# Two transformer blocks on one core: unnormalised x transposed between products, norm roots in the PSUM copies, alternating accumulators in the down projection

## What is computed

```python
for l in range(2):                                     # first block
    h = rms_norm(x, norm1_g[l])
    q, k, v, gu, gv = split(h @ w_in[l])               # 3584 columns
    ...                                                # attention, gelu(gu), gelu(gv), gating
    x = x + mixed @ w_o[l]
    h = rms_norm(x, norm2_g[l])
    g, u = split(causal_conv3(h @ w_up[l]))            # 2 x 5632 columns, 44 feature tiles each
    x = x + (silu(g) * u) @ w_down[l]
# second block: mod = silu(c) @ w_ada + b_ada (12288 columns), the same for c_ctx
hc = rmsnorm(ctx, norm1_w) * (1 + csc1) + csh1         # context stream, 256 tokens
s_f, s_b = ssd_branch(hc, ...)                         # states only
hl = rmsnorm(x, norm1_w) * (1 + sc1) + sh1             # x stream
x = x + g1 * token_mixer(hl, s_f, s_b)
x = x + g2 * sqrelu_mlp(rmsnorm(x, norm2_w) * (1 + sc2) + sh2)
out = rmsnorm(x, final_norm_w)
```

## Time and profile before

| | |
|---|---|
| median of 3 runs | 3853.71 us (3839.27 to 3853.76) |
| the profiled execution | 3845.48 us, its span 3843.7 us |
| TensorE (PE) busy | 3568.9 us, 93% of the span |
| VectorE (DVE) busy | 2363.7 us, 61% |
| ScalarE (ACT) busy | 1608.2 us, 42% |
| DMA | 687.60 MB, mean 179 GB/s |
| mean granted TensorE clock | 0.961 of full speed |

### The profile page before, as it was taken

How to read it: one execution, slowest core, us unless ns; L and a number is a source line. 1 busy time by engine, 2 the same in 40 slices (tenths; PEclk the granted TensorE clock), 3 DMA queues, 4 the chain that set the end, 5 groups by cost and what they waited for, 6 DMA issues and landing times.

```text
span 3843.7 us, 43309 instructions
## 1 busy us (share of the span) xinstructions
PE 3568.9 (93%) x16122; PEld 2908.9 (76%) x16122; DVE 2363.7 (61%) x2921; ACT 1608.2 (42%) x2106; POOL 26.4 (1%) x26
## 2 busy tenths in 40 slices
PE   6978999998898979999998898999988889999998
PEld 5766888887776867888886777787853678888887
DVE  4766788886555765677776556237665555555554
ACT  4443454554333453555554333224421344344443
POOL 0000000000000000000000000000000000000000
PEclk9989999999999989999999999979999999999999
DMA  6635577775666636577775664336600445656564
GB/s 209 185 110 201 181 226 225 231 229 180 192 224 210 194 114 219 181 229 233 232 229 184 193 235 148 85 104 198 186 1 0 159 144 189 188 190 187 191 189 149
DMA packets 357795, 687.60 MB, mean 179 GB/s; under 512 B 24591, under 2 KB 28704, under 8 KB 356384
## 3 DMA queue, kind: packets, MB, share of 16 engines
q1 hardware_dynamic: 357664, 685.82, 55.9%
HBM read 683.64 MB, written 2.10 MB: 178 GB/s over the span
## 4 chain that ended last, share of the span: by engine, by line
PE 61%; issue 20%; DVE 8%; DMA 5%; ACT 3%; DVEq 1%; SPq 1%; POOL 0%; ACTq 0%; POOLq 0%
PE acc L1836 14%; PE acc L1838 14%; PE acc L1837 14%; PE acc L2066 4%; PE acc L2067 4%; PE acc L2068 4%; DMA w_raw<-in_w_down 3%; DVE w_lo L1075 2%; DMA w_raw<-in_w_in 1%; DVE ada_sum L1150 1%; ACT w_hi L687 1%; PE turn L2006 1%; PE acc L2303 1%; DMA w_raw<-in_w_o 1%; PE side L2313 1%
## 5 line engine op out<-in xcount | busy, mean ns | idle before, releaser
L1075 DVE TENSOR_TENSOR w_lo<-w_raw,w_hi 128x1024 fp32r<-128x1024 f32 x708 | 843.1, 1222 | 500.9 <-ACT w_hi L687 462.3
L687 ACT ACTIVATE w_hi<-w_raw 128x1024 fp32r<-128x1024 f32 x708 | 744.1, 1061 | 970.3 <-DMA w_raw<-in_w_up 358.3
L1836 PE MATMUL acc<-w_hi,in_h 128*128 128x512 f32 x2112 | 840.6, 398 | 25.3 <-DVE w_lo L1075 14.0
L1838 PE MATMUL acc<-w_hi,in_l 128*128 128x512 f32 x2112 | 830.1, 393 | 0.0
L1837 PE MATMUL acc<-w_lo,in_h 128*128 128x512 f32 x2112 | 829.8, 393 | 0.0
L1836 PEld LDWEIGHTS acc<-w_hi,in_h 128*128 128x128 f32 x2112 | 401.9, 190 | 113.7 <-issue 21.0
L1838 PEld LDWEIGHTS acc<-w_hi,in_l 128*128 128x128 f32 x2112 | 401.0, 190 | 85.7
L1837 PEld LDWEIGHTS acc<-w_lo,in_h 128*128 128x128 f32 x2112 | 401.9, 190 | 81.5
L2066 PE MATMUL acc<-w_hi,in_h 128*128 128x512 f32 (+1 forms) x1024 | 408.1, 399 | 19.9 <-issue 8.2
L2067 PE MATMUL acc<-w_lo,in_h 128*128 128x512 f32 (+1 forms) x1024 | 402.7, 393 | 0.0
L2068 PE MATMUL acc<-w_hi,in_l 128*128 128x512 f32 (+1 forms) x1024 | 402.6, 393 | 0.0
(11 more groups left out here) (299 smaller groups left out, 3719.9 us busy)
## 6 DMA issues: line engine op xcount, KB each, us to landing
w_raw<-in_w_up SPq DMA_DIRECT2D x352, 512.0 KB, 3.8
w_raw<-in_w_mlp SPq DMA_DIRECT2D x256, 512.0 KB, 3.6
w_raw<-in_w_in SPq DMA_DIRECT2D x200, 512.0 KB, 3.8
w_raw<-in_w_ada SPq DMA_DIRECT2D x192, 512.0 KB, 4.6
w_raw<-in_w_down SPq DMA_DIRECT2D x176, 512.0 KB, 5.0
w_raw<-in_w_o SPq DMA_DIRECT2D x64, 512.0 KB, 4.4
w_raw<-in_w_out SPq DMA_DIRECT2D x32, 512.0 KB, 3.8
x_sb<-in_x SPq DMA_DIRECT2D x1, 2048.0 KB, 8.0
```

The source lines that it names most:

```text
L687: nc.scalar.activation(hi[s][:, ks], raw[s][:, ks], ACT.Copy).then_inc(w_hi[s][h], 1)
L1075: nc.vector.tensor_tensor(lo[s][:, ks], raw[s][:, ks], hi[s][:, ks].bitcast(F32), ALU.subtract).then_inc(w_lo[s][h], 1)
L1836: nc.tensor.matmul(acc[p][i][:], ah_[:, kt, tok], hi[s][:, k], start=(kt == 0), stop=False)
L1838: last = nc.tensor.matmul(acc[p][i][:], al_[:, kt, tok], hi[s][:, k], start=False, stop=(kt == ktn - 1))
```

## The change

1. **Roots in the copies.** x is transposed as it is, by plain transposes; `x_diag` and `turn_normed1` go. The gains are still applied per feature. The root of the token is a per-partition scale of the copy out of PSUM: the copies into `qk`, `v_sb`, `gv`, `gu` in *in*, and into `y` in *up*.
2. **Chunk by chunk.** In *o* the transposes of x for chunk c-1 stand after the first product of chunk c, with the gains behind it on ScalarE and VectorE; the last chunk's stand after the first product of *up*. In *down* of layer 0 the same is done for the next layer's *in*, after the third product of the next chunk. `n1_h`, `mix_h` and the like are new places, so that writing them does not touch operands in use. At the very start the gains come before the squares, between the first splits.
3. **Down.** Chunks alternate between `acc[0]` and `acc[1]`; `add_to_x` and `x_squares` of a chunk stand behind the first piece of the next. Chunk 0 takes its pieces in the order 8, 9, 0 to 7, 10, and `ah`, `al` are split two pieces ahead (the groups 8 and 9 lie clear of the *up* operands). The 12 `w_ada` pieces of a layer are 2, 4, 3, 3 per chunk instead of 3 each.
4. **Tables and context.** The next layer's tables are loaded at the end of *up* and transposed in *down*'s chunk 1, block 2's in layer 1. ctx is loaded before chunk 1 of layer 1, scaled by its roots in chunk 2, transposed and split beside chunk 3. Block 2 begins with the four ctx products of its first chunk, with the transposes of x (now scaled beforehand into `x_n`) between them; the x products on the same four pieces follow and free the slots.

The diff, cut to its core:

```diff
+    DN_ADA = [
+        {2: (32, 0), 3: (32, 1), 6: (33, 0), 7: (33, 1)},
+        {0: (34, 0), 1: (34, 1), 2: (35, 0), 3: (35, 1), 5: (36, 0), 6: (36, 1), 7: (37, 0), 8: (37, 1)},
...
+    DN_KT = [8, 9, 0, 1, 2, 3, 4, 5, 6, 7, 10]
...
+        def chunk_hi(l, u0, c, col, dst):
+            gained_hi(l, u0 + 2 * c, 4, col + 4 * c, lambda kt: dst(4 * c + kt))
...
+        layer_tables(0)
+        chunk_hi(0, U_N1, 0, T_N1, n1_high)
+        split_hi(0, 1)
+        chunk_hi(0, U_N1, 1, T_N1, n1_high)
+        split_hi(1, 1)
...
-                        nc.scalar.activation(qk[:, i, 2 * c:2 * c + 4].rearrange("p h d -> p (h d)"), src[:], ACT.Copy).then_inc(acc_free[p], 1)
+                        nc.scalar.activation(qk[:, i, 2 * c:2 * c + 4].rearrange("p h d -> p (h d)"), src[:], ACT.Copy, scale=root).then_inc(acc_free[p], 1)
...
+                    if n == 0 and c > 0:
+                        chunk_hi(l, U_N2, c - 1, T_N2, n2_high)
+                x_squares(l * AL[c % 2] + c // 2 * 2 + (1 + 8 + 2), c % 2, c, junk_o)
...
+                if before is None:
+                    chunk_hi(l, U_N2, 3, T_N2, n2_high)
+                    act_.wait_ge(rstd, l * 7 + 7)
...
-            for i in range(TT):
-                nc.vector.tensor_scalar(x_diag[:, i], ident[:], x_rstd[:, i:i + 1], None, ALU.mult).then_inc(xn_ready, 1)
...
+            act_lo(0)
+            act_lo(1)
+            for c in range(4):
                 for i in range(DN):
+                    if c == 0 and i == 1:
+                        finish_pair(NPAIR - 1)
+                    if c == 0 and i + 2 < DN:
+                        act_lo(i + 2)
                     split_lo(*later_place(l, "dn", c, i, 2))
+                    if i == 0 and c > 0:
+                        add_to_x(*product_place(l, "dn", c - 1, DN - 1), (c - 1) % 2, c - 1)
+                    if i == 2 and c > 0 and l == 0:
+                        chunk_lo(1, U_N1, c - 1, T_N1, 0, n1_low, n1_high)
...
+        def turn_x(l, u0, c):
+
+            for u in range(2):
+                turn(l, u0 + 2 * c + u, [x_sb[:, j, kt * P:(kt + 1) * P] for kt in (4 * c + 2 * u, 4 * c + 2 * u + 1) for j in range(TT)])
...
+                    if s == 0 and c > 0:
+                        pe.wait_ge(acc_free[1 - q], l * AL[1 - q] + (c + 1) // 2 * 2 + reads[1 - q])
+                        turn_x(l, U_N2, c - 1)
...
+                p = c % 2
+                if c > 0:
+                    pe.wait_ge(acc_free[p], l * AL[p] + c // 2 * 2 + down_reads[p])
...
+                    if l == 0 and c > 0 and i == 2:
+                        pe.wait_ge(acc_free[1 - p], l * AL[1 - p] + (c + 1) // 2 * 2 + down_reads[1 - p])
+                        turn_x(1, U_N1, c - 1)
...
+            if j == 0:
+                for n, s in pieces_of(j):
+                    pe.wait_ge(part2_lo, 2 * s + 2)
+                    product2(n, 4 * s, streams[1:], frees=False)
+                    if s > 0:
+                        turn_x2(2 * s - 2)
+                        turn_x2(2 * s - 1)
```

More of the change, by code:

```diff
@@ L2041, in _ @@
[L2041 to L2051 removed]
+            down_reads = [n + 2 * NPAIR for n in reads]
```

503 lines of the change are left out of this document (290 added, 213 removed), and 6 rows, old and new, of tables (DN_ADA, DN_ORDER).

## The result

The changed kernel takes 3697.39 us, median of 4 runs (3694.87 to 3704.94), against 3849.64 us for the kernel before in the same session: 0.9612 of it, 95% interval 0.9586 to 0.9637. The forecast was 3696 us, range 3668 to 3752. The profiled execution is the slowest of the four, 3704.94 us with a span of 3703.1 us, so a comparison of the two profiles shows 140.6 us of gain where the medians show 152.3. The changed kernel was profiled once more beside later experiments; that profile, with a span of 3694.1 us, is called the control.

A forecast was written before the change was run, and what follows sets the result against it. TensorE, busy 93% of the span, was taken as the bound, with time to win at its waits and slow restarts between stages. Gains less 4 us summed to 153 us off 3845.5, 3692, set at 3696 us toward the median; range 3668 to 3752.

The forecast's parts named there:

- The start, 14.4 us: Kernel start: first product at 31.1 us instead of 45.5, a gain of 14.4 us, bounds 8 and 18.
- Layer 0, o to up, 20.2 us: Seam from o to up's second product in layer 0: gain 20.2 us after 4.0 for a longer o, bounds 12 and 24.
- 1.0 us for each of three chunks: Layer 0's o: added cost per chunk from gains and remainders in the loop and TensorE's wait for the add.
- Layer 1, o to up, 19.9 us: Seam from o to up's second product in layer 1: second product at 1537.3 instead of 1557.2, bounds 12 and 22.
- Down, 27.3 and 23.7 us, and the seams behind it, 20.9 and 30.6: Gains in down of layers 0 and 1, then from down to the next in and between the blocks.
- the 3.5 us before the first matmul: Start of down: this wait of 3.5 us goes, since groups 8 and 9 can be split under up.
- Up's first pairs, -4: Up's first pair, whose third split waits for the root: a loss of 2 us in each layer, 4 us.
- The copies, 0: Scale operand on 120 copies out of PSUM: 9.6 us on ScalarE beside products, taken as 0, bounds 0 and 9.6.
- A: Rival: down stays paced by its loads, chunk 0 at 75 us, costing 32 us, total 3728; chance 0.20.
- B: Rival: short waits at 15 seams lower TensorE's clock, 2.0 us each, 30 us, total 3726; chance 0.11.
- C: Rival: down's piece loop slows to 8.3 us a piece, total 3900; chance 0.04 including outcomes up to no change.
- D: Rival: TensorE stands as long for adds or splits in three of four seams, losing 61 us of gains; chance 0.05.

The follow-up runs named there:

- Experiment 7: Changed kernel with VectorE in o making the w_ada sums one split earlier and the add to x ahead of a split; 3678.95 us, one run.
- experiment 6: Changed kernel with x transposed as a whole ahead of up's first product, roots still in the copies; 3716.31 us, one run.
- experiment 4: Changed kernel with no lead for the splits of act in down's chunk 0 instead of two pieces; 3733.24 us, one run.
- experiment 1: Changed kernel with the scale of all 120 copies out of PSUM replaced by the constant 1.0; 3690.22 us, 0.9599 of before.

## Why the prediction was right, and where not

*The start, 14.4 us:* right, 31.08 for 31.1; 13.4 to 14.2 us were left at the second chunk. The last steps of its working do not follow from each other (28.9 and four remainders of 0.48 give 30.8, not 30.4), but the mechanism is in the trace: ScalarE ends chunk 2 at 28.5 and VectorE at 30.2, and the transposes behind them end as the first product begins.

*Layer 0, o to up, 20.2 us:* 17.2, 18.4 in the control. The step that failed is "1.0 us for each of three chunks". *o* grew by 8.3 us (7.1 in the control) up to the start of its chunk 3 alone, where the prediction had 4.0 in all; the seam behind it gave 25.4 us (58.9 to 33.5) for the 24.2 that it had without them. Experiment 7 shows why *o* grew. The prediction named the loop and then priced only VectorE's extra work in it. It did not ask whose load the late split waits for: the slot comes free with the `w_ada` sums, so every wait in that loop is passed on through a load.

*Layer 1, o to up, 19.9 us:* 20.8. The mechanism is shown by experiment 6: 13.5 us of it is the chunk-wise work.

*Down, 27.3 and 23.7 us, and the seams behind it, 20.9 and 30.6:* together 109.2 measured (110.1 in the control) for 102.5. In layer 0 it was 50.7 for 48.2. Chunk 0 took 65.4 us for 66.0, and the cause named for it is shown by experiment 4. In layer 1 it was 58.5 for 54.3: all chunks took 61.5 to 64.5 us where I had given the first two 66 and the last 67. The step "the 3.5 us before the first matmul" failed: groups 8 and 9 can be split under *up*, but they stand in both streams behind the last split of the loop, and 3.39 us stayed. I had read that these groups lie clear of other operands, and not where their instructions stand.

*Up's first pairs, -4:* the two stretches gave +0.8 and -0.5 in the two profiles. No such cost shows.

*The copies, 0:* right, experiment 1.

*The sum, 153 us:* 161.2 up to block 2's second chunk. What no step had is that unchanged code could change: 11.6 us in the last MLP, where the loop no longer stays in TensorE's instruction memory, and 2.8 to 9.1 us in block 2, of which the larger figure comes with a lower clock. So the total was met partly by luck.

*The rivals.* A (loads pace *down*): chunk 0 took 65.4 and 63.2 us and chunk 1 63.5 and 62.9, not 75 and 70 or 76. B (clock at the seams): the granted clock was 0.99 and 1.00 over most of *down*,

```profile
955.00:1136.00 181.00, 178.53 (x805) 147.43 (x804) 113.02 (x121) 75.31 (x89) 0.00 (x0) 0.99 0.76 239
2030.00:2207.00 177.00, 174.79 (x798) 144.73 (x796) 120.27 (x137) 73.28 (x82) 0.70 (x1) 1.00 0.77 245
```

so the alternation did not lower it, and the sentence of the Trainium skill that the prediction set beside this rival ("TensorE: Matmul & The Clock Gate", section *A second HAM failure mode: psum-queue depth-cycling*) is not borne out by *down* here. Clock was lost, but elsewhere. C: 259.2 and 254.5 us for 88 pieces are 5.8 us a piece, far from 7.7. D: of the new waits only the 8.8 us for the add in *o* of layer 0 are of its kind.

## What to carry to other kernels

Where two engines prepare operands for a third, the part that is due next must stand at least one step ahead of any wait for a load. That one step was worth 40 us here; for the second no gain is shown. When a step is put into such a loop, follow the slot that it frees to the load and the split that wait for it, since that circle, not the step's own time, sets the cost. And compare unchanged stages too, with more than one profile of the same kernel: look up the same instruction in both profiles, stage by stage, and look at the instruction fetches of every hardware loop.

## What the runs showed of the hardware

A loop of TensorE with 1600 matmuls and weight loads in a pass ran its later passes without an instruction fetch or refetched every pass, 18 fetches of 16 KB in 360 us, by nothing but where it begins. In nine profiles of such placements TensorE then stood 3.0 to 3.8 us at each jump back, and the pass between the jumps took 182.9 us in the changed kernel instead of 177.7. In a tenth (experiment 6), refetched as well, it stood about 2.1 us and the pass took 180.2. A different length of the code ahead of it (192 matmuls fewer in the whole program) came with that, and naming the place of the loop's head undid it.

The granted clock after nearly the same two short waits (1.4, then 3.2 to 3.5 us) in the filter part was 1.00 in one execution and 0.50 in another of the same kernel. Over fourteen profiles the part of 284 us around it came out in two kinds, with 41 or 61.7 us at 1.2 GHz and 10 us apart, and the whole unchanged stretch moved by up to 14 us, more than most of the edits here.
